# Squares of the norm on ScalarE, and the first pair's transposes two items earlier, in a hybrid attention layer

## The reference

```python
h = jnp.einsum('bnd,de->bne', x, w_in)
qa, ka, va, ga, qb, kb, vb, gb = jnp.split(h, IN_SPLITS, axis=-1)
# mixer A: 8 heads, rotary, dilated sliding windows
out_a = _dilated_attention(_rope(qa), _rope(ka), va) * jax.nn.silu(ga)
# mixer B: 8 query heads, 2 key heads, normalised per head, then axial rotary
qb = _axial_rope(_rms_norm_heads(qb, q_norm), row, col)
kb = _axial_rope(_rms_norm_heads(kb, k_norm), row, col)
out_b = _gqa_attention(qb, kb, vb) * jax.nn.silu(gb)
f = jnp.einsum('bne,ed->bnd', jnp.concatenate([out_a, out_b], -1), w_out)
y = _layer_norm(DEEPNORM_ALPHA * x + f, ln_g, ln_b)
```

## Time and profile before

| what | us |
|---|---|
| median of three runs | 454.33 |
| profiled execution, its own time | 454.92 |
| its span | 452.9 |
| PE busy | 421.7 (93%) |
| DVE busy | 326.5 (72%) |
| ACT busy | 223.1 (49%) |
| POOL busy | 227.8 (50%) |

### The profile page before, as it was taken

One profiled execution on the slowest core, in us unless ns is written; L12 is line 12 of the kernel. 1 busy time (PEld: TensorE's weight loads), 2 busy tenths in 40 slices (PEclk: granted clock), 3 DMA queues, 4 the chain that ended last, 5 costly groups with the idle time before them and its releaser, 6 DMA issues.

```text
span 452.9 us, 8283 instructions
## 1 busy us (share of the span) xinstructions
PE 421.7 (93%) x2956; PEld 390.2 (86%) x2956; DVE 326.5 (72%) x858; ACT 223.1 (49%) x515; POOL 227.8 (50%) x286
## 2 busy tenths in 40 slices
PE   1999999799999999999999999998898999999990
PEld 1999998788999999998999999998797788888870
DVE  1478899956767786565777788665466887737997
ACT  3354223356746556675665555664657857621000
POOL 1046798762646537344247574751645977331111
PEclk9999999999999999999999999999899999999996
DMA  7814211220111102111011020007200060300222
GB/s 226 314 54 129 73 42 54 73 71 25 49 46 48 48 0 57 40 42 52 2 46 48 25 71 0 26 1 250 76 24 25 1 199 10 117 1 1 95 93 93
DMA packets 22585, 29.96 MB, mean 66 GB/s; under 512 B 1936, under 2 KB 16400, under 8 KB 22544
## 3 DMA queue, kind: packets, MB, share of 16 engines
q1 hardware_dynamic: 22112, 29.30, 20.5%
q10 hardware_dynamic: 432, 0.13, 0.1%
HBM read 26.28 MB, written 3.15 MB: 65 GB/s over the span
## 4 chain that ended last, share of the span: by engine, by line
PE 65%; DVE 18%; DMA 5%; issue 4%; POOL 3%; SPq 2%; ACT 2%; DVEq 0%; ACTq 0%; POOLq 0%
PE bank L561 14%; PE bank L563 14%; PE bank L562 14%; PE bank L523 9%; PE bank L636 7%; DVE tmp_s L812 3%; DMA raw<-w_out 3%; PE bank L596 3%; PE bank L597 3%; DMA h<-x_prompt 2%; DVE cst L1004 2%; DVE h L860 2%; DVE h L1012 2%; DVE h L1027 2%; DVE h L1003 2%
## 5 line engine op out<-in xcount | busy, mean ns | idle before, releaser
L561 PE MATMUL bank<-w_hi,t_lo 128*128 128x256 f32 (+1 forms) x528 | 162.6, 308 | 0.3 <-DVE h L833 0.3
L562 PE MATMUL bank<-w_lo,t_hi 128*128 128x256 f32 (+1 forms) x528 | 159.9, 303 | 0.0
L563 PE MATMUL bank<-w_hi,t_hi 128*128 128x256 f32 (+1 forms) x528 | 159.9, 303 | 0.0
L1057 POOL TENSOR_TENSOR w_lo<-raw,w_hi 128x512 fp32r<-128x512 f32 x59 | 78.1, 1325 | 67.5 <-ACT w_hi L693 67.5
L563 PEld LDWEIGHTS bank<-w_hi,t_hi 128*128 128x128 f32 x528 | 101.0, 191 | 3.9
L561 PEld LDWEIGHTS bank<-w_hi,t_lo 128*128 128x128 f32 x528 | 101.0, 191 | 3.8 <-DVE h L833 0.5
L562 PEld LDWEIGHTS bank<-w_lo,t_hi 128*128 128x128 f32 x528 | 101.1, 192 | 3.2
L1104 POOL TENSOR_SCALAR prob<-prob,den 128x512 f32<-128x512 f32 (+1 forms) x96 | 60.1, 630 | 49.6 <-DVE den L919 49.6
L748 ACT ACTIVATE p_hi<-bank 128x512 fp32r<-128x512 f32 x80 | 47.7, 596 | 53.4 <-PE bank L523 53.0
L739 ACT ACTIVATE prob<-prob,nmax 128x512 f32<-128x512 f32 (+1 forms) x96 | 62.0, 647 | 18.8 <-DVE nmax L898 18.5
L906 DVE TENSOR_TENSOR p_lo<-bank,p_hi 128x512 fp32r<-128x512 f32 x80 | 55.0, 688 | 20.7 <-ACT p_hi L748 20.2
(11 more groups left out here) (78 smaller groups left out, 677.1 us busy)
## 6 DMA issues: line engine op xcount, KB each, us to landing
raw<-w_in SPq DMA_DIRECT2D x51, 256.0 KB, 2.8
raw<-w_out SPq DMA_DIRECT2D x16, 256.0 KB, 4.8
h<-x_prompt SPq DMA_DIRECT2D x10, 256.0 KB, 3.7
y_prompt<-h SPq DMA_DIRECT2D x8, 256.0 KB, 2.0
h<-x_prompt SPq DMA_DIRECT2D x3, 512.0 KB, 8.5
h<-x_sample SPq DMA_DIRECT2D x2, 512.0 KB, 11.2
h<-x_sample SPq DMA_DIRECT2D x4, 256.0 KB, 5.7
y_sample<-h SPq DMA_DIRECT2D x4, 256.0 KB, 2.0
```

What stands on the lines that cost most here:

```text
L561: nc.tensor.matmul(out, a_lo, b_hi, start=(m == 0), stop=False)
L562: nc.tensor.matmul(out, a_hi, b_lo, start=False, stop=False)
L563: ins = nc.tensor.matmul(out, a_hi, b_hi, start=False, stop=end)
L1057: nc.gpsimd.tensor_tensor(w_slot(g)[1], raw_slot(g), w_slot(g)[0].bitcast(F32), ALU.subtract).then_inc(w_lo_pool, 1)
```

## The change

ACT now squares each of the 18 items of the norm itself, straight from the accumulator, ahead of its copy. The squares go to one of two halves of the tile `tanh` by turns, so ACT waits for the sums of two norms earlier (`summed`), and DVE's `sums` is the TENSOR_REDUCE alone. The three batches of the first pair move from places 19, 20, 21 to places 17, 18, 19 on PE, ACT and DVE (`STAGED_AT`). AHEAD is 22 before and after.

```diff
-ALONE = 19
+ALONE = 22
+STAGED_AT = 17
...
-        AHEAD = ALONE + len(first)
+        AHEAD = ALONE
...
+        def squares_of(n):
+            return tanh[:, HALF * (n % 2):HALF * (n % 2 + 1)]
...
-                if i >= ALONE:
-                    t_batch(first[i - ALONE])
+                if 0 <= i - STAGED_AT < len(first):
+                    t_batch(first[i - STAGED_AT])
...
+                    if KIND[c] == NORM:
+                        place, m = norms_of.index((c, n)), norm_heads(c) * HEAD_DIM
+                        if place >= 2:
+                            act.wait_ge(summed, place - 1)
+                        nc.scalar.activation(squares_of(place)[:, 0:m], accumulator(i)[:, 0:m], ACT.Square)
                     nc.scalar.activation(h[:, n, HOME[c]:HOME[c] + w], accumulator(i)[:, 0:w], ACT.Copy) \
                         .then_inc(act_evacuated, 1)
...
                 dve.wait_ge(*evac[i])
-                if n:
-                    dve.wait_ge(summed, n)
-                src = h[:, t, HOME[c]:HOME[c] + m * HEAD_DIM]
-                squares = tanh[:, 0:m * HEAD_DIM]
-                after(nc.vector.tensor_tensor(squares, src, src, ALU.mult))
+                squares = squares_of(n)[:, 0:m * HEAD_DIM]
```

More of the change, by code:

```diff
@@ L771, in _ @@
                     x_high(i + 1, 1)
-                if i >= ALONE:
-                    t_high(first[i - ALONE])
+                if 0 <= i - STAGED_AT < len(first):
+                    t_high(first[i - STAGED_AT])
                 for g in prepared[i]:
@@ L966, in _ @@
                     x_low(i + 1, 1)
-                if i >= ALONE:
-                    t_low(first[i - ALONE])
+                if 0 <= i - STAGED_AT < len(first):
+                    t_low(first[i - STAGED_AT])
                 for g in prepared[i]:
```

## The result

The changed kernel took 460.3 us (median of 7 runs, 458.97 to 461.11), the kernel before 455.29 in the same comparison (7 runs, 453.82 to 457.98). The ratio is 1.0081 with a 95% interval of 1.0054 to 1.0107, so by the ratio the change costs about 3.7 us. The two medians lie further apart, 5.0 us; of seven runs each they are the looser measure, and experiment 8 finds 1.0077 again. The profiled execution took 459.14 (span 457.1) against 454.92 (span 452.9), 4.2 more.

The account below looks back on a forecast made before the run. PE was taken to bound the kernel, losing 3.0 us where DVE was behind. Span 452.9 + 2.1 (stop) + 1.7 (clock) + 2.0 around it = 458.7, less 0.6 to the median: 458.1 us, range 454.6 to 460.2.

Parts of the forecast that it names:

- PE's new stop: Ahead of item 17 PE waits from 67.32 to 72.4 for POOL's add of rotation 11: 5.1 us.
- The old stops: PE's waits of 2.7 us for q_st and 0.3 for k_lo before the scores go: 3.0 us won.
- The clock: PE's granted clock falls to the lower level with the new stop: +1.7 us, ends 0 and 1.9.
- Rival 1: The new stop comes without the clock loss: 455.3 to 457.5 us, middle 456.4; chance 0.16.
- Rival 2: POOL's add ends early, at 68.0, so PE stops only 0.7 us: 452.0; break-even at 70.3; chance 0.12.
- Rival 3: ACT's new wait for sums two norms back holds a copy, PE finds no bank: about 460 us; chance 0.05.
- Rival 4: The shift is given back later, at a stop that doesn't follow PE: 454.3 us; chance 0.07.
- The squares' price: ACT's 18 squares cost 0.28 us each, covered by waits; DVE wins 5.5 to 8.1; neither enters the sum.
- The sum: Profiled span 452.9 + 2.1 stop + 1.7 clock + 2.0 around it is 458.7, less 0.6 to the median: 458.1.

Follow-up runs that it names:

- experiment 8: The changed kernel timed and profiled again with no edit: 459.55 us, ratio 1.0077 to the kernel before.
- experiment 6: Changed kernel with batches at items 18 to 20, POOL's doubled keys at place 15, values split at 16: 452.89 us, ratio 0.9942 to before.
- experiment 10: Changed kernel with batches at items 18 to 20 and POOL's split of the values at place 21: 453.77 us, ratio 0.9958 to before.
- experiment 5: Changed kernel with 44 extra matmuls, results unused, filling PE's stop ahead of the first batch: 457.49 us, ratio 1.0039 to before.
- experiment 11: Kernel before with 22 extra matmuls, results unused, at PE's stop near 316 us: 453.74 us, ratio 0.9952 to before.
- experiment 4: Changed kernel with POOL's doubled keys moved to place 15 and values split at 16, batches still at 17: 456.89 us, ratio 1.0027 to before.
- experiment 2: Changed kernel with the squares left on DVE, batches at items 17 to 19: 460.66 us, ratio 1.0117 to before.
- experiment 7: Changed kernel with batches at items 19 to 21, POOL's doubled keys at place 15, values split at 16: 453.75 us, ratio 0.9948 to before.
- experiment 3: Changed kernel with the batches one item later, at items 18 to 20: 454.88 us, ratio 0.9994 to before.
- experiment 9: Changed kernel with batches at items 19 to 21 and POOL's split of the values at place 21: 452.53 us, ratio 0.993 to before.

## Why the prediction came out right

**PE's new stop.** I had it at 5.1 us, it was 5.6: PE asked at 67.15 and not at 67.32, and POOL's add ended at 72.72, within 71.3 to 73.5 and 0.3 behind the 72.4 taken. Of the saving of 1.08, 0.94 is the earlier start; from there to the add's end it took 19.70 us where it had taken 19.84. POOL's rows ran some 0.8 shorter, but POOL waited 0.62 for DVE at 65.20. So the start was at the upper end of my range (0.26 to 0.9) and the run behind it near the lower (0 to 1.6). That the middle came out right is luck: two errors that cancel.

**The old stops.** 3.0 us were to go, and they went: no wait for q_st or k_lo is left. Experiments 6 and 10 show how close it is: with the batches one item later, 1.3 us for q_st are back in the one and none in the other.

**The clock.** +1.7 was expected, 1.96 lost in the profile, 1.8 by experiment 5. Stop and clock together put the scores 4.3 us later, where I had 2.1 + 1.7 = 3.8. Rival 1 (the stop without the clock, 2.1 us over before) is what experiment 5 makes on purpose: 1.8 over before by its ratio. It fails for the kernel as it stands. The step from which I took the clock, one fall behind 2.9 us and none behind 2.7, was thinner than it read: stops of this size go either way (below), and in experiment 11 the clock fell behind that very stop. So the kernel before has a clock loss of its own in some executions, which my sum left out; it makes the difference smaller, and may be why the ratio shows 3.7 and the profiles 4.2.

**Rival 2**, an early add, would have decided at 70.3. Experiment 4 brought the add to 70.56 by moving 2.6 us of POOL's own work, and even there the kernel is 0.3% slower than before, with the clock falling behind a stop of 3.6. The 70.3 weighed the stop at its length alone: PE would still have stood for 3.0 us there, and near 316 a stop of 2.9 had cost the clock. That POOL's queue and not DVE ends the wait is shown by experiment 4 (2.6 us of POOL's work out of the way, the add 2.2 earlier) beside experiment 2 against the change (8.1 us of squares in 256 columns off DVE, the add 1.75 earlier).

**Rival 3**: ACT's wait for the sums cost PE nothing; PE's only wait for ACT's h above 2 us is the one near 316. **Rival 4** is refuted: PE was busy through all of 92 to 234 as before, and the last matmul starts 4.5 us later (444.84 and 440.37). In the second profile of the changed kernel (experiment 8) the scores come 5.2 us later than before and the last matmul 3.1, as the part behind the stop near 320 varies; the whole span is 4.2 longer in both.

**The squares' price.** ACT's squares held it for 0.28 as taken. ACT is busy 3.9 us more in all, less than the 5 to 7 forecast; the squares' rows sum to 6.2, but rows that overlap count once, as at 44.59. DVE's busy time fell by 10.2, more than the 5 to 9 forecast: I had counted the twelve of 256 columns (8.1) and left out the six of 128. In the forecast I had weighed the Trainium skill (SBUF — State Buffer, Who interferes with whom), and inferred from its rule that the blocked time would pass to the next instruction with two SBUF inputs, so that DVE would win 5.5 of the 8.1. In sum it didn't pass: the squares of both widths had taken 10.7 us and DVE's busy time fell by 10.2. By groups it went both ways. L865 took 648 ns each where L860 took 770, and the products with sines 375 (L821) where they took 359 (L812). That page's rule says who can be blocked. How often it happens may depend on how tightly both queues are packed, and DVE's now had gaps; that is argued, not shown. In a single place the products were blocked by a lot. DVE's timeline of the changed kernel:

```profile
60.54 4.13 DVE L821 TENSOR_TENSOR tmp_s<-h,cst 128x64 f32<-128x64 f32 x4
```

The four products stood beside POOL's second v_st instruction, two w_lo and an add (60.32 to 64.6), and the twelve TENSOR_REDUCEs took 418 ns each on average, as before (420): nothing blocked them, as that page has it.

**The sum.** 458.1 was forecast, and +3.8 us; measured are 460.3 and +3.7 by the ratio, +4.2 in the profiles. As a bare time 460.3 is 2.2 above the forecast and 0.1 above the end of my range (460.2). The forecast stood on the 454.33 that I started from; the changed kernel set against that by the ratio (454.33 x 1.0081) is 458.0, 0.1 below it. Of the 2.2 us, 0.4 are the difference of the profiles (4.2 and not 3.8), 0.6 my step down from the profiled execution to the median, and 1.2 the distance of the changed kernel's median from its own profiled execution (459.14), for which I had nothing. In the first part the stop is 0.5 and the clock 0.3 more than I had, of which 0.2 is only that PE came to the stop earlier. The mechanism and the difference are right; that the difference agrees to 0.1 us is more than the forecast can take credit for.

## What to carry to other kernels

Before work is moved ahead on the engine that bounds the program, look up when its input is ready, and by which queue: here PE asked 8.5 us earlier and the add came 1.1 earlier, and the two items in between had been free cover. Taking work off a busy engine (DVE, 94%) did little for a wait that another engine ends (POOL, 91%), whose own queue had a chain of small instructions just ahead of the result. Count a stop of TensorE as its length and add what the clock can cost behind it: here 1.96 to 2.7 us behind stops of 3.6 to 6.4, and sometimes 1.5 behind one of 2.6. And try the two halves of a change apart: one was worth keeping.

## What the runs showed of the hardware

The clock behind a stop wasn't a function of the stop's length alone. Between 66 and 82 us all four stops of 3.6 to 6.4 us (experiment 4, after and again in 8, experiment 2) brought the granted clock to 0.50. Of the stops of 2.5 to 2.6 there, two did not (2.47 in the kernel before, 2.57 in experiment 3) and one did (2.59 in experiment 11), the first and the last in the same piece of program. Near 316, with the same items around the stop, the clock stayed 1.00 behind 2.4, 2.7 and 2.8 us (experiments 6, 9, 7) and fell to between 0.50 and 0.55 over 2 us behind the nine others of 2.2 to 3.4, the shortest of which is that of the changed kernel. What decides at 2 to 3 us stays open.

The price didn't follow the length either. From one batch to the next 2.7 us were lost behind a stop of 3.6, 1.96 and 2.3 behind 5.5 and 5.4, 2.1 behind 6.4 and 1.5 behind 2.6.

Small products on DVE can be held up far beyond their own length by POOL: 0.63 us for four of 128x64 beside POOL's small instructions, 1.61 beside one w_lo, 2.75 beside two v_st instructions and a w_lo, 4.13 beside one v_st, two w_lo and an add. POOL's POW held up nothing: in experiment 7 the four products at 77.09 took 0.63 inside a POW of 2.32 us (76.53 to 78.85), though both read two operands from SBUF. POOL's spans are rough, so this is an indication.
